# One-hots made five groups ahead of the row products, four output tiles side by side, states stored from a copy, norms squared chunk by chunk

## The reference, cut to what matters

```
layer 0: x = x + (h * gate) @ w_out          # recurrent block; h is a scan over time
layer 1: x = x + attention(x) @ w_o
each:    x = x + peer(rmsnorm(x))            # 8 heads, 16 of 16384 experts each
peer:    q = x @ wq; best 16 + 16 subkeys, best 16 of their sums -> expert numbers, gates
         out = sum_k gate_k * gelu(u[e_k] . x) * v[e_k]
end:     rmsnorm(x); also the last 3 pre-convolution rows, the last h, k and v
```

## Time and profile before

| what | value |
|---|---|
| median of 3 runs | 3487.92 us (3479.01 to 3489.25) |
| profiled execution, its own time | 3495.82 us |
| its span, first to last instruction | 3494.0 us |
| mean granted TensorE clock | 0.941 |
| PE busy | 3144.6 us (90%) |
| PE weight load busy | 2841.6 us (81%) |
| DVE busy | 2537.2 us (73%) |
| ACT, POOL busy | 1375.2 us (39%), 1642.7 us (47%) |
| DMA | 920.92 MB, mean 264 GB/s |

### The profile page before, as it was taken

The page is one execution under the profiler, slowest core; times in us unless marked ns, Lnnn a source line. Parts: engine busy times, 40 slices in busy tenths (PEclk is TensorE's granted clock), DMA queues, the critical chain, the costliest instruction groups (busy, mean ns, idle before and its releaser), DMA issues.

```text
span 3494.0 us, 46773 instructions
## 1 busy us (share of the span) xinstructions
PE 3144.6 (90%) x17262; PEld 2841.6 (81%) x17262; DVE 2537.2 (73%) x4945; ACT 1375.2 (39%) x2545; POOL 1642.7 (47%) x1157
## 2 busy tenths in 40 slices
PE   8768989898889999999888889997888889999997
PEld 7667989888889788888774689997888888888886
DVE  1834899865553799999667348999656545999996
ACT  2403333365555333333344133333555553333332
POOL 4432388766665434434130123786666654344331
PEclk9878999999999999999987799999999999999999
DMA  3272299788887999999220012897888879999993
GB/s 107 83 27 66 81 326 334 274 327 313 315 305 266 393 412 403 411 410 404 74 90 0 24 56 84 295 323 277 308 306 319 317 276 355 407 403 410 411 410 139
DMA packets 295107, 920.92 MB, mean 264 GB/s; under 512 B 36384, under 2 KB 86304, under 8 KB 291088
## 3 DMA queue, kind: packets, MB, share of 16 engines
q1 hardware_dynamic: 162864, 415.63, 34.6%
q0 software_dynamic: 111280, 404.77, 31.0%
q10 hardware_dynamic: 20736, 97.53, 7.0%
HBM read 817.34 MB, written 102.38 MB: 263 GB/s over the span
## 4 chain that ended last, share of the span: by engine, by line
PE 53%; DVE 24%; DMA 11%; POOL 5%; ACT 5%; issue 2%; SPq 0%; ACTq 0%; DVEq 0%; POOLq 0%
PE ps L1493 31%; PE ps L1391 10%; PE ps L1441 6%; DMA rowsA<-u,pick 6%; DMA rowsB<-u,pick 4%; POOL low L503 4%; DVE rowsA L981 3%; DVE rowsB L981 3%; ACT hotB L644 1%; PE ps L1376 1%; DMA hOut<-hlast 1%; DVE cand L1070 1%; DVE cand L1077 1%; ACT high L625 1%; PE ps L1473 1%
## 5 line engine op out<-in xcount | busy, mean ns | idle before, releaser
L625 ACT ACTIVATE high<-raw 128x1024 fp32r<-128x1024 f32 x512 | 541.5, 1058 | 883.2 <-PE ps L1493 686.1
L503 POOL TENSOR_TENSOR low<-raw,high 128x1024 fp32r<-128x1024 f32 x256 | 612.9, 2395 | 384.0 <-ACT high L625 381.3
L1441 PE MATMUL ps<-xh,high 128*128 128x384 f32 x2048 | 718.2, 351 | 26.1 <-POOL low L503 25.4
L1441 PE MATMUL ps<-xh,low 128*128 128x384 f32 x2048 | 700.8, 342 | 0.0
L1441 PE MATMUL ps<-xl,high 128*128 128x384 f32 x2048 | 700.3, 342 | 0.0
L1493 PE MATMUL ps<-high,hh 128*128 128x512 f32 x1536 | 483.9, 396 | 7.3 <-DVE low L1152 7.3
L1493 PE MATMUL ps<-low,hh 128*128 128x512 f32 x1536 | 481.5, 394 | 0.0
L1493 PE MATMUL ps<-high,hl 128*128 128x512 f32 x1536 | 480.7, 394 | 0.0
L1441 PEld LDWEIGHTS ps<-xh,high 128*128 128x128 f32 x2048 | 399.4, 195 | 33.1 <-POOL low L503 32.1
L1441 PEld LDWEIGHTS ps<-xl,high 128*128 128x128 f32 x2048 | 398.7, 195 | 0.0
L1441 PEld LDWEIGHTS ps<-xh,low 128*128 128x128 f32 x2048 | 396.2, 193 | 0.0
(11 more groups left out here) (254 smaller groups left out, 5201.7 us busy)
## 6 DMA issues: line engine op xcount, KB each, us to landing
raw<-uT SPq DMA_DIRECT2D x256, 512.0 KB, 6.4
raw<-v SPq DMA_DIRECT2D x256, 512.0 KB, 11.3
gate_dram<-gblk ACTq DMA_DIRECT2D x24, 2048.0 KB, 9.8
gt<-gate_dram SPq DMA_DIRECT2D x32, 1536.0 KB, 16.5
s_dram<-sring ACTq DMA_DIRECT2D x120, 384.0 KB, 6.3
sring<-s_dram SPq DMA_DIRECT2D x120, 384.0 KB, 12.0
raw<-wts SPq DMA_DIRECT2D x76, 512.0 KB, 3.7
rowsB<-u,pick POOLq DMA_INDIRECT x192, 7.3
```

The costliest lines, as they stand in the source:

```text
L503: pool.tensor_tensor(low[:, m % 4], raw[:, m % 4], high[:, (m + 2) % 3].bitcast(F32), ALU.subtract).then_inc(sem("lo_ready"), 1)
L625: act.activation(high[:, (m + 2) % 3], tile_raw(m), ACT.Copy).then_inc(sem("hi_ready"), 1)
L1441: ins = pe.matmul(ps[:, m % 2, 0:DN], w[:, c], x[:, c, 0:DN], start=(c == 0 and k == 0), stop=(c == NC - 1 and k == 2))
```

## The change

Seven things, in the order of the program:

- Norms 0, 1 and 3: DVE adds the squares of chunks 1 to 5 to chunk 0 as they come, and PE sums 3 chunks in place of 8. For norms 1 and 3 ACT squares a chunk as soon as its residual is added. `ones` holds 1/1024 and the root takes eps as bias, straight from PSUM; DVE's scale-and-add is gone.
- w_out: its first four tiles get buffers of their own (`outR`, `outL`, `outH`), are loaded early and split by POOL once the 16 input tiles are done. PE makes them side by side, chunk by chunk in 8 PSUM banks, each chunk as soon as its low half is there; the last four follow as before.
- The states: POOL copies them to `keepP`, `keepS`; SP stores the copies behind the query weights. DVE's wait for the three DMAs is gone. The two copies of caches go out later.
- `one_hots`: the first five groups are made with no rows used between them (HEAD_START = 5). GROUP0 goes from 53 to 55, 1.42 groups a tile; gathers 8 + 1.36 (m - 8), then 72 + 1.99 (m - 55). Two of the turns and one exponential move by one or two tiles.
- Norms 2 and 4: the sample part is folded and added first; ACT squares and PE sums inside `residual()`, sample tokens in 8 matmuls of 64, prompt in 8 of 512.
- Before the attention two key weights and the attention constants are loaded earlier.
- The final result is stored in four DMAs, two chunks each.

```diff
-EXP_S, EXP_T = 12, (22, 34, 54)
-TURN_T = (32, 52, 66)
-GROUP0, GROUPS_PER_TILE = 53, 1.4
+EXP_S, EXP_T = 12, (22, 34, 56)
+TURN_T = (32, 53, 68)
+GROUP0, GROUPS_PER_TILE = 55, 1.42
+HEAD_START = 5
...
-        n = 8 + 1.45 * (m - 8)
+        n = 8 + 1.36 * (m - 8)
-        n = 74 + 1.95 * (m - GROUP0)
+        n = 72 + 1.99 * (m - GROUP0)
...
 sync:
+                    if W_OUT <= w < W_OUT + OUTS:
+                        spq.dma_start(outR[:, w - W_OUT], wts[w]).then_inc(sem("out_loaded"), 16)
+                        continue
...
-            spq.dma_start(convP, xpre[:, :, TP:TP + CW - 1]).then_inc(sem("states_out"), 16)
-            spq.dma_start(convS, xpreS[:, :, :, TS:TS + CW - 1].rearrange("p c b k -> p (c b) k")
+            load_weights(W_PQ0, W_K)
+            spq.wait_ge(sem("state_kept"), 1)
+            spq.dma_start(convP, keepP[:, :, :]).then_inc(sem("states_out"), 16)
+            spq.dma_start(convS, keepS[:, :, :, :].rearrange("p c b k -> p (c b) k")
                           ).then_inc(sem("states_out"), 16)
             spq.wait_ge(sem("hlast_ready"), 1)
             spq.dma_start(hOut, hlast[:, :, :]).then_inc(sem("states_out"), 16)
-            load_weights(W_PQ0, W_K)
...
+            for c in range(0, NC, 2):
+                spq.wait_ge(sem("y_ready"), c + 2)
+                spq.dma_start(yT[:, c:c + 2], xn[:, c:c + 2]).then_inc(sem("out_done"), 16)
 gpsimd:
+                    if w == W_OUT:
+                        pool.wait_ge(sem("out_loaded"), 16 * OUTS)
+                        pool.wait_ge(sem("tile_done"), D_A)
+                    if W_OUT <= w < W_OUT + OUTS:
+                        f = w - W_OUT
+                        pool.tensor_copy(out_high(f), outR[:, f]).then_inc(sem("wh_ready"), 1)
+                        pool.wait_ge(sem("wh_ready"), splits_made(w))
+                        pool.tensor_tensor(outL[:, f], outR[:, f], out_high(f).bitcast(F32), ALU.subtract
+                                           ).then_inc(sem("w_split"), 1)
+                        continue
...
 scalar:
                 for c in range(NC):
+                    if s:
+                        act.wait_ge(sem("d_free"), (D_OUT, D_O)[s // 3] + c + 1)
                     act.activation(xn[:, c], xT[:, c], ACT.Square).then_inc(sem("sq_ready"), 1)
+                    if s and c >= NC - 2:
+                        high_weight(s // 3, c - NC + 2)
+                act.wait_ge(sem("sum_done"), s + 1)
+                act.activation(two(rinv[:, :]), halves(4), ACT.Sqrt, bias=eps[:, :]).then_inc(sem("rms_ready"), 1)
 vector:
+            def add_squares(s, c):
+                dve.wait_ge(sem("sq_ready"), SQ[s] + c + 1)
+                if c > 1:
+                    dve.wait_ge(sem("sq_added"), SUMMED * SUM_AT[s] + c - 1)
+                dve.tensor_tensor(xn[:, 0], xn[:, 0], xn[:, c], ALU.add).then_inc(sem("sq_added"), 1)
...
-                dve.wait_ge(sem("states_out"), 48)
...
                         ins.then_inc(sem("ones_made"), 1)
-                        dots(min(2 if g % 5 < 2 else 1, S0 + S1 - rows_done))
+                        if g >= HEAD_START:
+                            dots(min(2 if g % 5 < 2 else 1, S0 + S1 - rows_done))
 tensor:
+            def outputs():
+                pe.wait_ge(sem("d_free"), D_OUT)
+                pe.wait_ge(sem("w_split"), splits_made(W_OUT + OUTS - 1))
+                for c in range(NC):
+                    pe.wait_ge(sem("xl_ready"), X_OUT * NC + c + 1)
+                    for f in range(OUTS):
+                        a, b = out_high(f), outL[:, f]
+                        for j, (w, x) in enumerate(((a, xh), (a, xl), (b, xh))):
+                            for h in range(2):
+                                ins = pe.matmul(ps[:, dbank(D_OUT + f) + h, 0:H2], w[:, c],
+                                                x[:, c, h * H2:(h + 1) * H2],
+                                                start=(c == 0 and j == 0), stop=(c == NC - 1 and j == 2))
+                        if c == NC - 1:
+                            ins.then_inc(sem("tile_done"), 1)
+                for f in range(OUTS, NC):
+                    project_tile(W_OUT, D_OUT, f, X_OUT)
...
+                        if k == 0:
+                            pe.wait_ge(sem("sq_ready"), SQ[2 * l + 2] + 1)
+                            for c in range(NC):
+                                pe.matmul(ps[:, SUMS, 0:SMP], ones[:, :], xn[:, c, TP:T],
+                                          start=(c == 0), stop=(c == NC - 1))
+                        if k >= 5:
+                            prompt_sum(k - 5)
```

More of the change, by code:

```diff
@@ L89, in tiles_made, with loads_made @@
     return w + 1 + 2 * (NC - 1)
+OUTS = 4
+SQ = (0, NC, 2 * NC, 3 * NC + 1, 4 * NC + 1)
+SUMMED = NC - 3
+SUM_AT = {0: 0, 1: 1, 3: 2}
+def loads_made(w):
+    return (w if w < W_OUT else w - OUTS) // 2 + 1
 def splits_made(w):
@@ L205, in decoder @@
         mark = base.take("mark", [P, 1])
+        eps = base.take("eps", [P, 1])
+        keepP = base.take("keepP", [P, NC, CW - 1])
+        keepS = base.take("keepS", [P, NC, NB, CW - 1])
+        hlast = base.take("hlast", [P, NC, 1 + NB])
         raw_at = base.at
@@ L329, in dbank, with out_high @@
         def dbank(d):
-            return 2 * (d % 2)
+            return 2 * (d - D_OUT) if D_OUT <= d < D_OUT + OUTS else 2 * (d % 2)
+        def out_high(f):
+            return (outH[:, 0], outH[:, 1], high[:, 1], high[:, 2])[f]
         def wide(b):
@@ L476, in split_weights @@
                         continue
-                    if n >= 2:
-                        pool.wait_ge(sem("tile_done"), tiles_made(w - 2 if w - 2 not in (W_A, W_X) else w - 4))
+                    if w == W_K:
+                        pool.wait_ge(sem("mm_done"), after("mm_done", 0, 2 * KEYS))
+                    if w == W_OUT + OUTS + 1:
+                        pool.wait_ge(sem("tile_done"), D_OUT + OUTS)
+                    elif n >= 2 and w != W_OUT + OUTS:
+                        pool.wait_ge(sem("tile_done"), tiles_made(w - 2))
                     pool.tensor_copy(high[:, w % 2], raw[:, w % 2]).then_inc(sem("wh_ready"), 1)
@@ L813, in add_residual @@
                                       ).then_inc(sem("d_free"), 1)
+                    if 2 <= f < SUMMED + 2:
+                        add_squares(s, f - 1)
             def rg_lru():
                 dve.wait_ge(sem("params_loaded"), 16)
+                for c in range(1, SUMMED + 1):
+                    add_squares(0, c)
                 norm_stats(0)
@@ L1372, in sum_squares @@
                     pe.wait_ge(sem("ones_ready"), 1)
-                for c in range(NC):
-                    pe.wait_ge(sem("sq_ready"), NC * s + c + 1)
+                pe.wait_ge(sem("sq_added"), SUMMED * (SUM_AT[s] + 1))
+                for c in (0, NC - 2, NC - 1):
+                    if c:
+                        pe.wait_ge(sem("sq_ready"), SQ[s] + c + 1)
                     for h in range(2):
@@ L1500, in residual @@
                     pe.wait_ge(sem("a_copied"), after("a_copied", l, 1))
+                    for c in range(NC):
+                        ins = pe.matmul(ps[:, ACC, c * SMP:(c + 1) * SMP], accS0[:, c * P:(c + 1) * P], fold,
+                                        start=True, stop=True)
+                    ins.then_inc(sem("fold_done"), 1)
                     for k in range(NC):
                         if k >= 4:
-                            pe.wait_ge(sem("y_added"), after("y_added", l, k - 3))
+                            pe.wait_ge(sem("y_added"), after("y_added", l, k - 2))
                         for c in range(4):
```

98 lines of the change are left out of this document (57 added, 41 removed).

## The result

The changed kernel takes **3307.88 us** (median of 4, 3303.82 to 3310.29) against 3483.47 (3475.54 to 3489.25) of the kernel before, run beside it: a ratio of **0.9497, 95% interval 0.9478 to 0.9517**. The forecast was 3288 with a range of 3255 to 3345. The profiled execution took 3303.82 us, its span is 3302.0.

The account below looks back on a forecast made before the run. No engine was full in the gate stage: PE waited on late gathers and one-hots, elsewhere on a chain of waits. Gains of 144.8 + 43.4 + 12.0 = 200.2 us from 3495.8 gave 3295.6, median 3288 us, range 3255 to 3345.

Parts of the forecast that it names:

- the rival of the DMA engines: Rival: DMA engines bind the gate stage, which would need 371 GB/s; kernel at 3307 to 3331 us, chance 0.22.
- gate stages, with the way to the first group: Both layers' gate stages: the head start of one-hots removes most of PE's waits, gaining 144.8 us.
- recurrent output: From the recurrent output to norm 1: its reciprocal begins at 238.6 in place of 282.06 us, 43.4 us less.
- norm 0: First norm: 12 records in place of 32 end near 17.2, root at 17.9 against 19.36; 1.4 us less.
- norms 2 and 4: Norms after the down tiles: PE's sum stays, only DVE's 0.77 us go; 0.5 us less each.
- The ideal of 365.5 us: Gate stage, first to last group, without waits: 67 up tiles and 96 groups, 280.1 + 85.4 us.
- The 12 us of waits left per layer: Gate stage: waits expected to remain, 12 us a layer, one for each of the twelve stores.
- 3.5 groups of 3.83 us, 13.4 us of cover, against a wait of 8.91 us: Gate stage: 4.7 groups ahead leave 13.4 us of cover for PE against a gather wait of 8.91 us.
- No lead: Rival: the gate stage's lead does not hold, PE waits for each gather again; kernel at 3428 us, chance 0.12.
- POOL at a full ring: Rival: in the gate stage POOL stands at a full ring, delaying low halves; 3498 us or more, chance 0.04.
- three take some 12: Recurrent output: POOL's three more splits take some 12 us and fit its idle time of 20.34 + 11.45 us.
- The 21.7 us for the states: Recurrent output: part of the 43.4 us gain, from no longer waiting for the states' DMA.

Follow-up runs that it names:

- undo_onehots: The changed kernel with HEAD_START = 0 and the five old lines of the gather and group tables; 3453.84 us, ratio 0.994 to the kernel before.
- groups_from_58: The changed kernel with groups from tile 58 at 1.5 a tile and gathers at 2.1 a tile from there; 3268.08 us, ratio 0.9404.
- head2: The changed kernel with a head start of 2 groups in place of 5; 3336.05 us, ratio 0.9584 to the kernel before.
- head0: The changed kernel with HEAD_START = 0 in place of 5, keeping the new tables; 3707.52 us, ratio 1.0661 to the kernel before.
- pad_352: The changed kernel with 352 unused bytes behind its new small tiles, shifting later buffers 1536 bytes in place of 1184; 3294.10 us, ratio 0.947.
- states_alone: The kernel before with only the states part: POOL copies, own tiles, DMAs behind the weights' loads, no DVE wait; 3471.24 us, ratio 0.9986.

## Why the prediction was right, and where it was not

The time fell in the range and on the side that was forecast, but its nearness is in part luck. By the profiled executions the gain is 192.0 us (3495.82 to 3303.82) against a sum of 200.2, and in it the gate stages gave 27 us more than forecast and all other terms together 36 less. From median to median it is 175.6 us, since the profiled execution of the kernel before stands 12.4 us above its median. The other 12 us of the miss against 3288 are the executions: the profiled one of the changed kernel is 4.1 below its median, where the forecast set it 7.9 above. And 3308 lies where the rival of the DMA engines was put, though not for that rival's reason.

| term | forecast | measured |
|---|---|---|
| gate stages, with the way to the first group | -144.8 | -172.2 |
| recurrent output | -43.4 | -36.8 |
| norm 0 | -1.4 | +11.0 |
| norm 3 | -6.6 | -5.9 |
| norms 2 and 4 | -1.0 | -1.8 and +3.8 |
| output DMAs | -3.0 | -4.1 |
| down stages | 0 | +14.2 |

The small remainders (gates to down, norm to `up(0)`) are -0.5 together.

**Gate stages: right mechanism, wrong residue.** The ideal of 365.5 us was right, the stage takes 368.2. The 12 us of waits left per layer were too many: 2.7 are left. They were counted as one for each store of gates, but the trace of the kernel before has 40 waits of ACT for one-hots in the stage. Against the two single profiles the term is 27 us too small; against undo_onehots, which isolates it, 154.0 stand where 144.8 were forecast. The wait ahead of the first group did not shrink by the 8.4 us of two more tiles: it is 13.3 us in place of 13.55. Only the three further tiles of groups_from_58 took it away. **The step that failed is the reasoning about cover**: "3.5 groups of 3.83 us, 13.4 us of cover, against a wait of 8.91 us". The lead itself is there, 2 to 5 groups at the starts of all up tiles but the last (0 to 2 in the kernel before, until its last tiles), but it works by opening the loop through ACT's and POOL's order. The same arithmetic put head2 at 3430 (measured 3336) and head0 at 3500 at most (measured 3707). I had the link that closes the loop in view, ACT's and POOL's order, and used it only for the rival.

**DMA engines bind (0.22): did not come.** The needed 371 GB/s were moved (368), and later runs moved 378 and 385 with PE at work throughout. The gathers did land later, as the rival said, and nothing waited for it. By the Trainium skill (DMA: Bandwidth & Descriptors, Where 436 GB/s comes from), some 358 GB/s is the HBM limit of a core; the 391 GB/s of pad_352's down stage speak against it as a limit for one core that runs alone. **No lead (0.12)** and **POOL at a full ring (0.04)** did not come either: POOL waits 3 us for row slots in the stage, and up tiles start on time.

**Recurrent output: the step that failed is the one that sets POOL's three more splits ("three take some 12") against POOL's own idle time alone.** They fit POOL's time and not DVE's. The gates were done 8.0 us later, with norm 0's 11.0 taken out; 2.1 came back because ACT instead of DVE then sets the pace up to the first product, and the tiles and the sum took 57.7 us from the first low half in place of 56.9. 8.0 - 2.1 + 0.7 = 6.6 us, the miss. With the splits moved the stage takes 219.1 us, 43.6 less than before, and the forecast was 43.4. The 21.7 us for the states were 23.0 alone; the tiles side by side and the shorter sum were not run alone, so the rest is read from the chain. The first `uT` loads were not delayed, as forecast: from norm 1's reciprocal to `up(0)` it is 127.6 us, before 127.8.

**Norm 0: the step that failed is "12 records in place of 32 end near 17.2".** It began the sum at the last square. The change puts five adds on DVE ahead of it, and they stand behind DVE's wait for the parameters (until 14.98), which cost nothing as long as DVE's next work came at 17.85. From there they ran beside POOL's first splits, and ACT's table load came behind its waits, at 28.28, where it stood at 12.97 in the kernel before. I had counted the adds at the other norms and not looked at what stands ahead of them on DVE here.

**Down stages: a cost that the sum does not have.** The new small tiles move every later buffer by 1184 bytes, and the term, put at nothing, is 14.2 us. No row of the profile before could show this; but the stage ran at a DMA share of 0.98, and I did not ask what would make its transfers longer.

**The small terms** held within 1.3 us but for norm 4, whose products ran at the lower of the two clock levels (3.66 us for the 16 of L1604, where norm 2 took 1.98; granted clock 0.50 from 3270 to 3280). The gain at norm 2 is luck too. From the last down tile to the reciprocal it is 20.8 us in the kernel before, at both norms and a granted clock of 0.92. The twelve runs with the new `residual()` have 24 such stretches: six take 18.9 to 19.0 us at a clock of 1.00, the other 18 take 23.0 to 24.7 at 0.72 to 0.78. So this edit, forecast as a gain of 0.5 us each, mostly costs 2 to 4. PE stands still some 2.5 us behind the last down tile at norm 2 and at norm 4 of the changed kernel alike; what decides the clock there stays open.

## What to carry to other kernels

Where a late transfer delays work that itself stands ahead of issuing the next transfer, follow the orders of all engines round until they close. In such a loop a small lead can be worth far more than its length: here a head start of two groups, 7.7 us of PE's work, took the stage from 567 to 384 us. For every instruction that a change adds, ask what wait stands ahead of it on its engine and which operations of another engine will run beside it, not only whether its own engine has idle time. After adding even a small buffer, compare the landing times of large transfers in stages that the change does not touch.

## What the runs showed of the hardware

**Buffer addresses and transfers.** The kernel places its tiles one behind the other from byte 16512 of each partition on. By their sizes, `raw2` (half of the `v` tiles) stands at 204032 in the kernel before and at 205568 in pad_352, both multiples of 256, and so does `gt`. With 1184 bytes it stands 160 past one, with the 1152 of states_alone 128 past one. The first two have down stages of 537 to 538 us, states_alone of 545 and 547, and the runs with 1184 bytes of 542 to 546. `raw` and the row slots stand 192 past a multiple in both of the first, so it is not every buffer that must be aligned. The Trainium skill (DMA: Bandwidth & Descriptors, How a descriptor splits into AXI transactions) says that where a descriptor does not start at a multiple of 256 bytes, its first transaction starts at the boundary below, and the bytes before the start still cost time on the bus. It tells this of reads, and here the moved buffers are written, so it may fit but is not shown. What the runs show is that shifts of 1184 and 1152 bytes cost and one of 1536 does not. No run here moved one buffer alone, so which of them counts, and what the step is (1152 is a multiple of 128, 1536 also one of 512), stays open.

**DVE beside POOL.** The last column of the convolution by shape, in the changed kernel (mean ns of one):

```profile
L928 DVE SCALAR_TENSOR_TENSOR xc<-xpreS,prm,xc 128x64 f32<-128x64 f32 x3 | 7.1, 2359 | 0.0
L928 DVE SCALAR_TENSOR_TENSOR xc<-xpre,prm,xc 128x512 f32<-128x512 f32 x3 | 4.3, 1420 | 0.1
L925 DVE TENSOR_SCALAR xc<-xpreS,prm 128x64 f32<-128x64 f32 x1 | 2.3, 2342 | 0.0
```

In the kernel before they took 277, 751 and 308 ns. The small ones now last about as long as one of POOL's subtractions (2.4 to 2.7 us). That looks like a wait for a whole instruction of POOL's and not like a share of speed, and the short DVE instructions lose most. The Trainium skill (SBUF — State Buffer, Who interferes with whom) says this of a DVE instruction with two SBUF inputs beside a POOL instruction that reads SBUF, and of DVE's two-port modes; the rows agree. Both sides pay: POOL's cast went from 1.04 to 1.56 us where they met at norm 0.
